# One-hot comparisons with an operand in PSUM, all lower gate halves on GpSimd, and waits moved behind tile loads

## The reference, cut to what matters

```python
def peer_ffn(h, w_q, sub_keys, u_tab, v_tab):
    ...
    idx = jnp.take_along_axis(cand_i.reshape(...), best_pos, axis=-1)   # 8 heads x 16 experts a token
    gate = jax.nn.softmax(best_s, axis=-1)
    def expert_block(inp):
        hb, ib, gb = inp
        act = jax.nn.gelu(jnp.einsum('bpd,bphkd->bphk', hb, u_tab[ib]), approximate=False)
        coef = (act * gb).astype(hb.dtype)
        return jnp.einsum('bphk,bphkd->bpd', coef, v_tab[ib])
```

## Time and profile before

| | us |
|---|---|
| median of three runs (2278.05 to 2283.14) | 2282.73 |
| the profiled execution | 2281.69 |
| its span | 2279.9 |

### The profile page before, as it was taken

The page is one execution under the profiler, slowest core; times in us unless marked ns, Lnnn a source line. Parts: engine busy times, 40 slices in busy tenths (PEclk is TensorE's granted clock), DMA queues, the critical chain, the costliest instruction groups (busy, mean ns, idle before and its releaser), DMA issues.

```text
span 2279.9 us, 27268 instructions
## 1 busy us (share of the span) xinstructions
PE 2137.2 (94%) x10296; PEld 1675.8 (74%) x10296; DVE 1462.7 (64%) x2308; ACT 926.5 (41%) x1527; POOL 1047.4 (46%) x828
## 2 busy tenths in 40 slices
PE   8999999999999999999999988787888699999999
PEld 6877767468787667878787766666666588888887
DVE  6456175442337742248989599999995366666665
ACT  4223354642333233013344466566664444433342
POOL 6555654304232217778588877777775300000000
PEclk9999999999999999999999999999999799999999
DMA  5221322202011112232166545556667688888884
GB/s 202 86 78 71 130 68 88 73 28 84 32 43 56 56 38 93 93 129 93 56 194 210 188 147 213 199 211 232 217 206 260 249 288 291 289 288 288 289 287 160
DMA packets 98291, 359.32 MB, mean 158 GB/s; under 512 B 8480, under 2 KB 41504, under 8 KB 73328
## 3 DMA queue, kind: packets, MB, share of 16 engines
q1 hardware_dynamic: 98160, 357.56, 45.4%
HBM read 286.09 MB, written 71.30 MB: 157 GB/s over the span
## 4 chain that ended last, share of the span: by engine, by line
PE 66%; DVE 18%; POOL 8%; issue 5%; ACT 3%; DMA 1%; SPq 0%; DVEq 0%; POOLq 0%; ACTq 0%
PE ps L1434 10%; PE ps L1435 10%; PE ps L797 9%; PE ps L798 9%; PE ps L799 9%; POOL wring_parts L2621 5%; DVE area L2505 2%; PE ps L1244 2%; PE ps L786 2%; PE ps L1381 2%; PE ps L1382 2%; DVE area L2489 2%; DVE area L2408 2%; DVE area L2490 2%; DVE area L2405 1%
## 5 line engine op out<-in xcount | busy, mean ns | idle before, releaser
L1381 PE MATMUL ps<-sqbuf_parts,wring_parts 128*128 128x512 f32 x1024 | 423.4, 413 | 23.7 <-POOL wring_parts L2621 23.7
L2621 POOL TENSOR_TENSOR wring_parts<-wring_parts,wring 128x512 fp32r<-128x512 f32 x256 | 380.8, 1515 | 136.9 <-ACT wring_parts L1852 136.9
L2577 POOL CAST wring_parts<-wring 128x512 fp32r<-128x512 f32 x236 | 169.6, 759 | 546.1 <-PE ps L799 429.1
L1382 PE MATMUL ps<-normed_x_parts,wring_parts 128*128 128x512 f32 x1024 | 413.8, 404 | 0.0
L2581 POOL TENSOR_TENSOR wring_parts<-wring,wring_parts 128x512 fp32r<-128x512 f32 x244 | 351.4, 1471 | 6.6 <-ACT wring_parts L1848 1.5
L1381 PEld LDWEIGHTS ps<-sqbuf_parts,wring_parts 128*128 128x128 f32 x1024 | 200.7, 196 | 70.8 <-POOL wring_parts L2621 23.4
L1382 PEld LDWEIGHTS ps<-normed_x_parts,wring_parts 128*128 128x128 f32 x1024 | 200.1, 195 | 43.3
L1884 ACT ACTIVATE area<-area,rt 128x128 bf16<-128x128 bf16 x512 | 162.6, 390 | 135.2 <-DVE area L2489 135.2
L797 PE MATMUL ps<-resid_parts,wring_parts 128*128 128x512 f32 (+1 forms) x528 | 201.9, 382 | 6.2 <-DVE normed_x_parts L2005 3.3
L798 PE MATMUL ps<-normed_x_parts,wring_parts 128*128 128x512 f32 (+1 forms) x528 | 197.6, 374 | 0.0
L799 PE MATMUL ps<-resid_parts,wring_parts 128*128 128x512 f32 (+1 forms) x528 | 196.8, 373 | 0.0
(11 more groups left out here) (269 smaller groups left out, 4546.9 us busy)
## 6 DMA issues: line engine op xcount, KB each, us to landing
wring<-in_weights_dram SPq DMA_DIRECT2D x65, 1024.0 KB, 4.8
wring<-in_uT_dram SPq DMA_DIRECT2D x128, 512.0 KB, 4.2
area<-in_vT_dram SPq DMA_DIRECT2D x44, 1024.0 KB, 6.7
hidden_table<-area SPq DMA_DIRECT2D x32, 1024.0 KB, 6.5
gate_table<-area SPq DMA_DIRECT2D x32, 1024.0 KB, 7.5
area<-gate_table SPq DMA_DIRECT2D x32, 1024.0 KB, 9.0
wring<-in_vT_dram SPq DMA_DIRECT2D x20, 1024.0 KB, 6.9
rt<-hidden_table SPq DMA_DIRECT2D x32, 512.0 KB, 4.6
```

Source lines behind the costliest of these rows:

```text
L1381: pe.matmul(out, first[:, d], h_first[:, k, :], start=(k == 0), stop=False)
L1382: mm = pe.matmul(out, rest[:, d], h_rest[:, k, :], start=False, stop=(k == KD - 1))
L2577: ins = nc.gpsimd.tensor_copy(up[:, d, :], W(name)[:, d, :])
L2621: ins = nc.gpsimd.tensor_tensor(rest[:, a:a + PIECE], first[:, a:a + PIECE], u_raw[t % len(USLOT)][:, a:a + PIECE], ALU.subtract)
```

## The change

`BESIDE` goes from 18 to 17, so the 128 quads are dealt to tiles 44 to 111 instead of 44 to 115 (8 of the tiles then get one quad, 58 two). A copy of `iota` is put into PSUM bank 7 by ScalarE, and both comparisons read it there. The quads' products go to three banks, 4 to 6. VectorE, ScalarE and GpSimd prepare quad n + 3 when quad n is due (`LEAD`). All lower halves are made by GpSimd. On SP a piece's first store goes out one tile later, behind the next U load; the rest of the last piece is stored at tile 112; the waits for the stores and the loads for the combine stand at tile 121, behind the last U load.

```diff
--- before.py
+++ after.py
@@ -63,7 +63,7 @@
 PIECES = T // HALF
 
 
-BEFORE, BESIDE = 11, 18
+BEFORE, BESIDE = 11, 17
 QUADS = T // 4
 
 
@@ -80,6 +80,7 @@
 TILES = EG * GROUPS
 USLOT = (1, 2, 3, 5, 0, 4)
 STORES = 4
+LEAD = 3
 
 
 HALVES = 2 * GROUPS
@@ -439,6 +440,8 @@
         bsum = view(at + 5248, TT, HP)
         entT = rt[:, :, :].rearrange("p a b -> p (a b)")[:, 0:3 * T].rearrange("p (a b) -> p a b", a=3)
 
+
+        iota_ps = ps[:, 7, 0:P]
         hot_ring = view(16384, 4096).bitcast(BF16).rearrange("p (z q t n) -> p z q t n", z=4, q=4, t=4)
         oneA, oneB = hot_ring[:, 0], hot_ring[:, 1]
         gateB = view(18432, 2048).bitcast(BF16).rearrange("p (q t z n) -> p q t z n", q=4, t=4, z=2)
@@ -533,7 +536,8 @@
         stored = [sem(f"stored{i}") for i in range(2)]
         hot_second = sem("hot_second")
         hot_gates = sem("hot_gates")
-        odd_low = sem("odd_low")
+        gates_low = sem("gates_low")
+        places_copied = sem("places_copied")
         gates_rounded = sem("gates_rounded")
         gates_split = sem("gates_split")
         places_hot = sem("places_hot")
@@ -613,7 +617,7 @@
 
         def spread_out(n):
 
-            return ps[:, 4 + n % 4, :].rearrange("p (t n) -> p t n", t=4)
+            return ps[:, 4 + n % 3, :].rearrange("p (t n) -> p t n", t=4)
 
         block = ctx.enter_context(nc.Block())
 
@@ -716,14 +720,15 @@
                     load_u(t + len(USLOT))
                 if j == 0 and g:
                     store_hidden(g - 1)
+                if parts:
+                    store_piece(*parts.pop(0))
                 for n in quads_at(g, j):
                     if (n + 1) % (QUADS // PIECES) == 0:
                         parts += [(n // (QUADS // PIECES), part) for part in range(STORES)]
-                if parts and (n != QUADS - 1 or not quads_at(g, j)):
-                    store_piece(*parts.pop(0))
-                if t == EG * (BEFORE + BESIDE) - 1:
+                if t == EG * (BEFORE + BESIDE):
                     while parts:
                         store_piece(*parts.pop(0))
+                if t == TILES - len(USLOT) - 1:
 
                     sp.wait_ge(stored[0], 8 * PIECES * STORES)
                     load_v(0)
@@ -1399,11 +1404,10 @@
                 q = n % 4
                 pe.wait_ge(hot, n + 1)
                 pe.wait_ge(hot_gates, n + 1)
-                if n % 2:
-                    pe.wait_ge(odd_low, n // 2 + 1)
-
-                if n >= 4:
-                    pe.wait_ge(copied, n - 3)
+                pe.wait_ge(gates_low, n + 1)
+
+                if n >= 3:
+                    pe.wait_ge(copied, n - 2)
                 for j in range(4):
                     pe.matmul(spread_out(n)[:, j, :], oneA[:, q, j, :], gateB[:, q, j, 0, :], start=True, stop=False)
                     mm = pe.matmul(spread_out(n)[:, j, :], oneA[:, q, j, :], gateB[:, q, j, 1, :], start=False, stop=True)
@@ -1908,16 +1912,17 @@
                                ).then_inc(turned_copied, 1)
             act.wait_ge(turned_copied, TT)
             act.activation(w_hi, entT[:, 2, :], ACT.Copy).then_inc(gates_rounded, 1)
+            act.activation(iota_ps, C("iota"), ACT.Copy).then_inc(places_copied, 1)
             act.wait_ge(gates_split, 1)
-            weigh_gates(0)
-            weigh_gates(1)
+            for n in range(LEAD):
+                weigh_gates(n)
             for g in range(BEFORE, BEFORE + BESIDE):
                 for j in range(EG):
                     gelu(g, j)
                     beside(EG * g + j)
                     for n in quads_at(g, j):
-                        if n + 2 < QUADS:
-                            weigh_gates(n + 2)
+                        if n + LEAD < QUADS:
+                            weigh_gates(n + LEAD)
             for g in range(BEFORE + BESIDE, GROUPS):
                 for j in range(EG):
                     gelu(g, j)
@@ -2482,18 +2487,12 @@
                 def across(key):
                     return entT[:, key, tokens].unsqueeze(2).to_broadcast([P, 4, P])
 
-                iota = C("iota").unsqueeze(1).to_broadcast([P, 4, P])
+                iota = iota_ps.unsqueeze(1).to_broadcast([P, 4, P])
                 if n >= 4:
                     dve.wait_ge(spread, n - 3)
                     dve.wait_ge(hot_gates, n - 3)
                 dve.tensor_tensor(oneB[:, q], iota, across(1), ALU.is_equal).then_inc(hot_second, 1)
-                ins = dve.tensor_tensor(oneA[:, q], iota, across(0), ALU.is_equal)
-                if n % 2:
-                    ins.then_inc(hot, 1)
-                    return
-                dve.wait_ge(hot_second, n + 1)
-                dve.tensor_tensor(gateB[:, q, :, 1, :], oneB[:, q], w_lo[:, tokens].unsqueeze(2).to_broadcast([P, 4, P]),
-                                  ALU.mult).then_inc(hot, 1)
+                dve.tensor_tensor(oneA[:, q], iota, across(0), ALU.is_equal).then_inc(hot, 1)
 
             def add_quad(n):
                 piece, i = n // (QUADS // PIECES), n % (QUADS // PIECES)
@@ -2530,11 +2529,12 @@
             dve.wait_ge(turned_copied, TT)
             dve.wait_ge(gates_rounded, 1)
             dve.tensor_tensor(w_lo, entT[:, 2, :], w_hi, ALU.subtract).then_inc(gates_split, 1)
-            for n in range(2):
+            dve.wait_ge(places_copied, 1)
+            for n in range(LEAD):
                 one_hots(n)
             for n in range(QUADS):
-                if n + 2 < QUADS:
-                    one_hots(n + 2)
+                if n + LEAD < QUADS:
+                    one_hots(n + LEAD)
                 add_quad(n)
             split_v(0)
             split_v(1)
@@ -2634,23 +2634,24 @@
                     for split in range(split + 1, split + 8):
                         split_u(split)
 
-            def low_of_odd(n):
+            def low_gates(n):
 
                 pool.wait_ge(hot_second, n + 1)
                 if n >= 4:
                     pool.wait_ge(spread, n - 3)
                 w = w_lo[:, 4 * n:4 * n + 4].unsqueeze(2).to_broadcast([P, 4, P])
-                nc.gpsimd.tensor_tensor(gateB[:, n % 4, :, 1, :], oneB[:, n % 4], w, ALU.mult).then_inc(odd_low, 1)
-
-            for t in range(split + 1, TILES):
-                split_u(t)
+                nc.gpsimd.tensor_tensor(gateB[:, n % 4, :, 1, :], oneB[:, n % 4], w, ALU.mult).then_inc(gates_low, 1)
+
+            for t in range(split + 1, TILES + 4):
+                if t < TILES:
+                    split_u(t)
                 if t == EG * BEFORE + 3:
                     pool.wait_ge(gates_split, 1)
-                    low_of_odd(1)
-                if t >= 4:
-                    for n in quads_at((t - 4) // EG, (t - 4) % EG):
-                        if n % 2 and n + 2 < QUADS:
-                            low_of_odd(n + 2)
+                    for n in range(LEAD):
+                        low_gates(n)
+                for n in quads_at((t - 4) // EG, (t - 4) % EG):
+                    if n + LEAD < QUADS:
+                        low_gates(n + LEAD)
 
 
 
```

## The result

| | before | after |
|---|---|---|
| median of the runs, us | 2282.82 | 2177.35 (2176.14 to 2181.49) |
| profiled execution, us | 2281.69 | 2177.73 |
| its span, us | 2279.9 | 2175.9 |
| ratio to before | | 0.9546 (0.9528 to 0.9564) |

On another chip the same kernel came to 0.9553 (0.9527 to 0.9579). The change takes 105 us away; 78 were forecast, and 2177 lies under the range.

The account below looks back on a forecast made before the run. VectorE was taken to bound the gate stage, GpSimd after the change. 1665.8 + 16 x 3.71 (59.4) + 1 + 4.9 + 470.5 gave a 2201.6 us span, so 2204.4 us; range 2190 to 2240.

Parts of the forecast that it names:

- Part 2: Gate stage, all lower halves on GpSimd: 1.40 us each, a tile's split 2.53 us, 348.7 us of GpSimd work.
- GpSimd is the new bound: Gate stage: GpSimd needs 348.7 us, 37 us over the next engine, and so sets the pace.
- rival (d): Gate stage: GpSimd starves TensorE in every tile, clock drops, collisions stay; 64 tiles from about 1338, in all 2321 us; 3%.
- The sign that I had named for a wrong forecast: Gate stage: GpSimd showing idle time; expected were GpSimd busy over 95% and TensorE waiting in most tiles.
- The loop of Part 3: Gate stage, Gelu to split, lower half, quad and hidden tile: 10.08 us for two tiles, 0.6 us slack against GpSimd's 10.66.
- rival (a): Gate stage: the loop takes over, 5.6 instead of 5.25 us a tile over 64 tiles, +22 us, so 2227; 15%.
- the wait of ScalarE for its first V tile: End of tile 121: ScalarE's first V rounding waits some 7 us, with no stall of TensorE.
- the gap ahead of the combine: Between hidden tiles and combine: V rounding, coefficient rounding and its split stay a chain, put in at 4.9 us.
- The 16 last tiles: From tile 112 to the end of the hidden tiles: 16 x 3.71 (59.4) us, plus 1 us for a U load.
- Rival (c): Gate stage: one-hots still collide with GpSimd, which needs 406 us; lower halves end at 1722.6, in all 2262 us; 7%.
- (b): Start of the combine: late V tiles hold it, the gap grows by 12 us, so 2216; 10%.
- Part 2's other half: Gate stage: VectorE loses 64 lower halves of 1.136 us each, leaving its need at most 312 us.

Follow-up runs that it names:

- e1: The changed kernel with both comparisons reading iota from SBUF again: 2272.03 us, 0.9963 of the kernel before.
- e7: The changed kernel with the second comparison (oneA) reading iota from SBUF, the first from PSUM: 2206.75 us, 0.9666 of the kernel before.
- e5: The changed kernel with GpSimd's lower halves ahead of the split of the U tile in each step: 2163.78 us, 0.9486 of the kernel before.
- e4: The changed kernel with two quads ahead instead of three: 2210.77 us, 0.9696 of the kernel before.
- e6: The changed kernel with the even lower halves made by VectorE again: 2175.90 us, 0.9522 of the kernel before.
- e2: The kernel before with iota in PSUM and three banks for quads: 2211.04 us, 0.9687 of the kernel before.
- e3: The kernel before with SP's new order only, quads left on 72 tiles: 2268.10 us, 0.9938 of the kernel before.
- e8: The changed kernel with the quads dealt to 72 tiles instead of 68: 2178.85 us, 0.9552 of the kernel before.

## Why the prediction was wrong

The direction and the order of the parts were right; the size was not. The span was put at 2201.6 and is 2175.9, 25.7 us less. Tile 112 begins at about 1640.4 and not at 1665.8, 25.4 us earlier. So the whole miss lies in one stretch, and by its own steps it goes like this.

**The step that failed is the price of a lower half in Part 2.** It was taken as 1.40 us with 1.36 and 1.48 as ends; it is 1.04. The ends came from the rows of before, and every one of these 64 instructions started while a VectorE instruction with two SBUF inputs was running. I wrote that down ("it has not been seen without two-input work") and still let the shortest row be the lower end of the range. Worse, I took the row at 1509.58 as nearly free of the collision because the one-hot beside it had its short length of 0.67 us. It had started first:

```profile
1509.43 0.67 DVE L2490 TENSOR_TENSOR area<-cst,rt 128x512 bf16<-128x512 f32 x1
```

It ran on for 0.52 us after the lower half's start at 1509.58, and the lower half took 0.38 us over its 1.04. So it goes in all 64: what each took over 1.04 us is what the VectorE instruction running at its start still had to run, less 0.14 us (0.136 to 0.145), by the starts and ends in the trace of before. The other way round it is the same: the 243 one-hots of e1 that started while GpSimd ran took over their free 0.675 us what GpSimd's instruction still had to run, less 0.13 (0.06 to 0.13). The first keeps its time, as the 58 lower halves of e7 do; the second waits. Both seemed to lose because back to back they take turns. In e1 the lower half of 1505.10 waits for the one-hot of 1504.82, the one-hot of 1505.61 for that lower half, the next lower half for that one-hot.

Of this the Trainium skill's page "SBUF — State Buffer", section "SBUF: two separate sides", has the rule: of a GpSimd instruction and a VectorE instruction with two SBUF inputs, the one that starts first holds the shared port pair for its whole length and the other is fully blocked. The prediction set it aside for the sizes ("here both lose"). The traces agree with it, sizes too (the 0.14 and 0.13 us above are what is left over). So a meeting adds a wait to an instruction and does not stretch it by a factor, and the price could therefore be had from before: a split's two pieces take 3.44 us in the crowd and 2.54 outside, 0.45 a piece, and 1.47 less 0.45 is 1.02.

**What followed from it.** 128 x 0.36 = 46 us of GpSimd's work were never there. With the measured 2.04 us for a pair of them and 2.50 from a split's start to the next instruction its need is 128 x 1.02 + 67 x 2.50 = 298 us, under TensorE's 309, so "GpSimd is the new bound" was wrong. Had the rest of the sum gone on with the loop's own 9.70 us for two tiles from rival (d)'s 1338 on, tile 112 would have stood at 1648, 17 of the 25 us; the others lie mostly at the stage's start, since tile 48 begins near 1332 in the trace. The sign that I had named for a wrong forecast, idle time of GpSimd inside the stage, is in the trace (90% busy, not 95), and TensorE waits 26 times in 66 tiles, not in most.

**The loop of Part 3** was right in every link. With 1.02 in the place of 1.40 its 10.08 us become 9.70; the trace has 9.79 and 9.82 for two tiles. As a rival (a) it was there only as a loss; in fact it caught the gain: without it the stage would have been shorter by another 16 us (e5, 5 of them at its start). e4 confirms it from the other side.

**Right as put:** the one-hots (0.69 forecast, 0.68 measured), the split (2.53 forecast, 2.55 for its two pieces), the rule of the Trainium skill's page "SBUF — State Buffer", section "Who interferes with whom", that at most one SBUF input keeps a VectorE instruction out of GpSimd's way (with it the traces agree: of the 256 comparisons after and the 128 from PSUM in e7 none takes over 0.71 us), the wait of ScalarE for its first V tile (7 forecast, 7.11 measured), the gap ahead of the combine (4.9 against 4.9), the combine (470.5 against 469.5). The 16 last tiles take 61.1 us (60.4 forecast).

**Rival (c)**, collisions that stay, was put at 2262; e1 is that case and has 2272. Rivals (b) and (d) did not come. Part 2's other half, work taken off VectorE, was counted as part of the gain; e6 shows it as none at this pace.

**Where the 105 us come from.** iota in PSUM alone 70 (e2), SP's order alone 13 (e3), the third quad of lookahead 33 on top of the rest (e4); they overlap, since each is measured in another surrounding. Nothing that can be told from zero comes from the move of the lower halves (e6) nor from the 68 tiles (e8).

## What to carry to other kernels

When two engines lengthen each other's instructions, no row from inside that crowd is a lower bound for either. Ask of each row what the other engine was running when it started, and take that one's rest off; the short length of one does not say that the other was spared, it may just have come first. Once an overloaded engine is relieved, work out the loop of waits with the new durations first: here it, and not the next engine's load, set the pace, and turning the order of two steps on GpSimd was worth another 14 to 16 us. An operand that every instruction of a hot loop reads is worth a bank of PSUM if that leaves it one SBUF input.

## What the runs showed of the hardware that was not expected

- GpSimd's multiplication of 128 x 512 (bf16 by a broadcast value) takes 1.03 to 1.05 us alone and 1.35 to 1.51 when it starts while VectorE runs an instruction with two SBUF inputs (e7, e1); its subtraction of 128 x 512 in float32 takes 1.26 to 1.30 alone and 1.60 to 1.81 in e1.
- A meeting costs only the one that starts second, and costs it what the first still has to run, less 0.12 to 0.14 us in most cases (before, e1, e7). The first is not lengthened: at 1509.43 before, the one-hot kept its 0.67 us while GpSimd took 1.42 for 1.04, and in e7 58 lower halves kept 1.03 to 1.04 while a one-hot waited.
- VectorE's comparison with one operand in PSUM costs 0.68 us, the same as with both in SBUF and nobody beside it.
